# Q and k chunks of pairs 1 and 2 as block products ahead of attention, half the fill pieces, and a new order inside an attention step

## The chip, the cores and the metric

The kernel runs on one core of a Trainium2 chip, in one launch. The metric is the device time in microseconds; the kernel before took 1108.95 us, the median of three runs (1108.9 to 1109.0).

## What is computed

One layer of a trunk over x (1024 tokens, 1024 features, float32): a token mixer, then a SwiGLU network, each between two RMS norms with a residual. Cut to the part around the change:

```python
h = rms_norm(x, g_pre_mix)
hc, bg, cg, q, k, v = split(h @ w_in, 6)          # each 1024 tokens x 512
y_conv = bg * causal_conv3(cg * hc)               # 512 channels
y_attn = band_attention(q, k, v, rel_bias)        # 8 heads of 64, chunks of 64 tokens,
                                                  # each sees itself and 8 chunks to the left
y = [group_norm(y_conv), group_norm(y_attn)] @ w_out
x = x + rms_norm(y, g_post_mix)
x = x + rms_norm((silu(gate) * up) @ w_ffn_out, g_post_ffn)   # gate, up from rms_norm(x) @ w_ffn_in
```

## The kernel before

Every float32 operand of a large product is split into a high part (rounded to the matmul's format, by ScalarE) and a low part (the rest, by VectorE), and a product takes three passes: high x high, high x low, low x high. A chunk is 128 output channels for all 1024 tokens, so plainly it takes 8 slices of the contraction x 3 passes x 2 halves of the tokens = 48 matmuls of 512 columns.

**Stages.** First v is projected, while the normed x is transposed. Then come FRONT = 6 rounds (`front_multiply`). A round makes two chunks at once with seven block products in place of eight (a Strassen-Winograd scheme: the 2 x 2 blocks are the two chunks' weights in two halves of the contraction, and the even and odd token tiles in two halves of it). A block product is 12 matmuls, a round 84, where two plain chunks take 96. The sums of weights (`front_sum`) and of results (`bank_sum`: u2, u3, c22, c21, c12) are VectorE's; ScalarE makes the high parts (`front_high`), VectorE the low ones (`front_low`). Rounds 0 to 4 make the conv's inputs and gates, round 5 q and k of head pair 0. Conv statistics and transposes of three conv channels groups (`stats`, `norms`) lie between products of rounds 4 and 5. Then comes the attention of four pairs of heads, t = 0 to 3 (PAIRS = 4, LAST = 3), then the output projection, the FFN in block products, and the end.

**The attention.** A pair has 9 steps (s = 0 to STEPS - 1), and 8 tiles of 128 queries. The band of a tile has up to 640 keys (tiles 4 to 7; fewer for the first ones). A unit u is one head of a tile. For each tile:

- TensorE `scores(t, i)`: q times k in three passes, both heads side by side in the array, into PSUM.
- VectorE `add_bias(t, u)`: adds the bias, takes the maximum, writes scores to SBUF (`biased` counts units).
- ScalarE `exp(t, u)`: the exponential and its sum (`exp_done`).
- TensorE `transpose_p(t, i)`: the weights turned, into PSUM; ScalarE `read_pT` copies them to SBUF (`pT_act`), for 640 keys VectorE copies the fifth block (`pT_dve`).
- TensorE `output(t, i)`: tiles i and i + 1 times v, after both are copied; VectorE `copy_o`, TensorE `turn_back`, VectorE `read_o` bring them to their place. ScalarE `squares` sums squares of o for its norm, `o_norm`, `o_scale`, `o_finish` and `transpose_o` finish the norm one pair later.

Each engine's queue is written out by hand in its own `step(t, s)`, and works in that order. A wait holds all that stands behind it on its engine.

**Fill.** The q and k chunks of pairs 1 to 3 and two chunks of the conv's last group (c and b) are not made in rounds but in 64 pieces of 6 matmuls (`piece`), laid between the steps of the attention: AHEAD = 3 before the first step, and FILLS per step. Four pieces make half a chunk, in one PSUM bank. `half_bank()` is free again when a reader has copied the half out (`read_half`, semaphores `half_free`), so the first piece of a half waits for that copy. ScalarE copies halves of q and k into rows QN and KN, VectorE multiplies the conv's into CU and CV. `high_in` and `low_in` split the weights of the next chunk, `high_q`, `low_q`, `high_k`, `low_k` split the next pair's q and k for its scores (`qk_ready`).

**Queues.** SP issues the loads of weights (`load_front`, `load`), the stores and loads of v (`store_v`, `load_v`) and of the three finished conv groups (`store_conv`, `load_conv`), in program order, each behind its semaphore. GpSimd's queue brings the bias and raises the norms' means to the power -1/2.

TensorE's step before, cut:

```python
if s in (3, 5, 7):
    output(t, s - 3)
if scored(t, s):
    pe.wait_ge(biased, unit(t, 2 * s))
    for i in scored(t, s):
        scores(t, i)
...
pe.wait_ge(exp_done, unit(t, 2 * s))
transpose_p(t, s - 1)
for q in range(pieces_ahead(t, s), pieces_ahead(t, s + 1)):
    piece(q)
```

## Time and profile before

| | |
|---|---|
| median of 3 runs | 1108.95 us |
| the profiled execution | 1108.85 us, span of its instructions 1106.8 us |
| granted clock of TensorE | 1.00 over the span |
| TensorE busy | 1096.4 us, 99% of the span, 5653 matmuls recorded |
| VectorE, ScalarE, GpSimd busy | 764.7, 480.4, 160.4 us |
| chain that ended last | TensorE 97%, ScalarE 1%, DMA 1% |
| DMA | 164.11 MB, mean 148 GB/s |

The span is what the rows' times count in; the execution's own time is 2.05 us longer. A busy time of TensorE counts matmuls from start to a modelled end, which overlap, so the distance between two starts tells what one costs. The chain is followed back from the last instruction; since it is TensorE nearly throughout, the time is TensorE's work and its waits. The rounds lie from 60.28 to 183.40 us, the attention from there to 367.30.

### The profile page before, as it was taken

To read this page: it belongs to the slowest core of one execution; us is meant where nothing else is said; L and a number is where in the kernel's file an instruction comes from. 1 tells how busy PE (TensorE), PEld (TensorE's weight loads), DVE (VectorE), ACT (ScalarE), POOL (GpSimd) and SP (SyncE) were. 2 spreads that over 40 slices of the span, in tenths; PEclk is the share of its full clock that TensorE was granted. 3 is DMA by queue.
4 is the path that set the end of the run, shared out by engine and by line. 5 is a ranking of instruction groups with operands and counts; after the bars stand their busy time and mean duration, and the time that the engine had idled before them with its cause. 6 is when DMAs were issued, how large, how long until landed. Compare 5 with 4: busy or idle time off the path is not lost.

```text
span 1106.8 us, 16172 instructions
## 1 busy us (share of the span) xinstructions
PE 1096.4 (99%) x5653; PEld 908.6 (82%) x5653; DVE 764.7 (69%) x1267; ACT 480.4 (43%) x911; POOL 160.4 (14%) x258
## 2 busy tenths in 40 slices
PE   8999999999999999999999999999999999999997
PEld 7888887878878888888888888888888888888886
DVE  6878855455656756868777777878787777555584
ACT  6542233666665655734323232323223257444441
POOL 2300022010101220312112211211221110000031
PEclk9999999999999999999999999999999999999999
DMA  7332216300100444535546445543644689677632
GB/s 273 110 119 71 58 57 230 113 20 21 38 2 20 160 163 135 171 96 172 159 145 208 135 123 187 177 146 114 218 136 150 212 304 385 235 232 223 219 115 79
DMA packets 116183, 164.11 MB, mean 148 GB/s; under 512 B 7752, under 2 KB 73304, under 8 KB 116128
## 3 DMA queue, kind: packets, MB, share of 16 engines
q1 hardware_dynamic: 98496, 103.30, 29.2%
q0 software_dynamic: 16464, 55.89, 14.5%
q10 hardware_dynamic: 1168, 4.20, 1.0%
q8 instruction: 33, 0.54, 0.2%
q14 instruction: 22, 0.18, 0.1%
HBM read 119.56 MB, written 46.94 MB: 150 GB/s over the span
## 4 chain that ended last, share of the span: by engine, by line
PE 97%; ACT 1%; DMA 1%; DVE 0%; issue 0%; SPq 0%; DVEq 0%; POOL 0%; POOLq 0%
PE psum L1280 34%; PE psum L1307 18%; PE psum L874 12%; PE psum L1113 10%; PE psum L1164 8%; PE psum L1025 4%; PE psum L917 3%; PE psum L898 2%; PE psum L888 2%; PE psum L863 1%; PE psum L1001 1%; DMA arena<-in_x 1%; PE psum L925 0%; PE psum L1007 0%; PE psum L907 0%; ACT arena L1516 0%
## 5 line engine op out<-in xcount | busy, mean ns | idle before, releaser
L1280 PE MATMUL psum<-arena_r,ws 128*128 128x512 f32 x960 | 224.1, 389 | 0.0
L1280 PEld LDWEIGHTS psum<-arena_r,ws 128*128 128x128 f32 x960 | 180.3, 188 | 37.3
L1280 PE MATMUL psum<-hT,ws 128*128 128x512 f32 x720 | 169.9, 389 | 0.0
L1280 PEld LDWEIGHTS psum<-hT,ws 128*128 128x128 f32 x720 | 135.1, 188 | 27.9
L874 PE MATMUL psum<-hT,ws 128*128 128x512 f32 (+1 forms) x624 | 142.3, 380 | 0.4 <-ACT arena L1542 0.4
L1307 PE MATMUL psum<-hT 128*128 128x512 f32 (+1 forms) x600 | 135.2, 385 | 0.0
L1307 PEld LDWEIGHTS psum<-hT 128*128 128x128 f32 x600 | 111.3, 188 | 22.5
L874 PEld LDWEIGHTS psum<-hT,ws 128*128 128x128 f32 x624 | 107.9, 189 | 20.0 <-issue 0.8
L2401 DVE TENSOR_TENSOR misc<-misc,psum 128x512 f32<-128x512 f32 x100 | 68.4, 684 | 49.1 <-PE psum L1280 45.7
L1724 ACT ACTIVATE ws<-o_raw 128x512 fp32r<-128x512 f32 x40 | 25.1, 627 | 139.2 <-DVE o_raw L2379 138.7
L1164 PE MATMUL psum<-ws,hT 128*128 128x512 f32 x348 | 81.7, 393 | 0.0
L1307 PE MATMUL psum<-ws 128*128 128x512 f32 (+1 forms) x348 | 78.1, 382 | 0.0
L1164 PEld LDWEIGHTS psum<-ws,hT 128*128 128x128 f32 x348 | 64.5, 188 | 13.5 <-issue 0.3
L1307 PEld LDWEIGHTS psum<-ws 128*128 128x128 f32 x348 | 63.9, 188 | 12.6
L1724 ACT ACTIVATE ws<-raw 128x512 fp32r<-128x512 f32 x80 | 49.7, 623 | 39.2 <-PE psum L1280 38.3
L1113 PE MATMUL psum<-arena_r,ws 128*128 128x512 f32 x276 | 65.5, 391 | 0.0
L1113 PEld LDWEIGHTS psum<-arena_r,ws 128*128 128x128 f32 x276 | 51.4, 188 | 10.6
L2396 DVE TENSOR_TENSOR ws<-raw,ws 128x512 fp32r<-128x512 f32 x80 | 55.1, 690 | 6.7
L2475 DVE TENSOR_TENSOR hT<-arena,hT 128x512 fp32r<-128x512 f32 x62 | 40.0, 687 | 19.9 <-ACT hT L1771 19.5
L1357 ACT ACTIVATE misc<-arena 128x1024 bf16<-128x1024 f32 (+2 forms) x37 | 34.8, 941 | 40.8 <-DVE arena L2527 16.6
L1771 ACT ACTIVATE hT<-arena 128x512 fp32r<-128x512 f32 x62 | 35.6, 624 | 36.8 <-PE psum L1307 29.8
L1113 PE MATMUL psum<-hT,ws 128*128 128x512 f32 x216 | 51.2, 390 | 0.0
(262 smaller groups left out, 1578.0 us busy)
## 6 DMA issues: line engine op xcount, KB each, us to landing
raw<-in_w_ffn_in SPq DMA_DIRECT2D x44, 512.0 KB, 4.4
act_scratch<-arena POOLq DMA_DIRECT2D x77, 256.0 KB, 3.2
raw<-in_w_in SPq DMA_DIRECT2D x22, 512.0 KB, 3.9
arena<-in_w_ffn_out POOLq DMA_DIRECT2D x22, 512.0 KB, 5.7
arena<-act_scratch SPq DMA_DIRECT2D x38, 256.0 KB, 3.5
arena<-in_x SPq DMA_DIRECT2D x16, 512.0 KB, 6.7
raw<-in_w_out SPq DMA_DIRECT2D x16, 512.0 KB, 3.3
raw<-act_scratch SPq DMA_DIRECT2D x26, 256.0 KB, 3.2
```

The costliest lines, as they stand in the source:

```text
L874: last = mm(PP[pair][:, at:end] if to is None else to, w[wp], hT[:, hp, k, at:end], start=(k == 0 and (wp, hp) == (0, 0)), stop=(k == KT - ...
L1025: last = mm(v_bank(i), hT[:, hp, k, i * P:(i + 1) * P], v_weights(wp, k), start=(k == 0 and part == 0), stop=k == 7 and part == (1 if i < ...
L1113: last = mm(blocks(front_bank(n, i)), w[:, k * P:(k + 1) * P], b_operand(i, part, k), start=fresh_bank and k == 0 and w is hi and part == ...
L1164: last = mm(pair[:, half * 512:(half + 1) * 512], a, ws[:, slot, wp, half * 512:(half + 1) * 512], start=(first is not None and a is hi an ...
L1280: last = mm(blocks(bank), w[:, k * P:(k + 1) * P], b_operand(i, part, k), start=fresh_bank and k == 0 and w is hi and part == 0, stop=k == ...
L1307: last = mm(bank[:, at:end], a[:, n * P:(n + 1) * P], b[:, at:end], start=fresh_bank and a is ah and b is bh, stop=i == NP - 1 and a is al ...
L1357: go(dst, src, ACT.Square, scale=scale, accum_out=acc).then_inc(done[0], 1)
L1724: go(w_op(i)[0], w_raw[i], ACT.Copy).then_inc(w_hi, 1)
L1771: go(out_op(c, part)[0], raw_ring[c % RING][:, part * 512:(part + 1) * 512], ACT.Copy).then_inc(out_hi, 1)
L2396: tt(lo, w_raw[i], hi.bitcast(F32), ALU.subtract).then_inc(w_split, 1)
L2401: tt(out, a, bank, ALU.add).then_inc(made, 1)
L2475: tt(lo, raw_ring[c % RING][:, part * 512:(part + 1) * 512], hi.bitcast(F32), ALU.subtract).then_inc(out_split, 1)
```

## The change

- FRONT_PAIRS = 3: q and k of pairs 1 and 2 are made in two more rounds, in the order pair 2, pair 1, pair 0 (FRONT = 8). Their results are staged in rows 18 and 17: ScalarE stages one block (`stage_c11`), VectorE writes the other three; SP stores them to DRAM (`store_qk`) and reads them back, behind v, into rows of their own (`load_qk`, QK_ROWS).
- FILLED = 4 chunks are left for fill: q and k of pair 3, and the conv's last c and b. That is 32 pieces: AHEAD = 4, none in steps 0 to 2 of pairs 0 and 1, none in steps 0 and 1 of pairs 2 and 3.
- TensorE's step: scores stand first; the output of two tiles behind them; the last output of a pair moves behind the next pair's first scores; in step 8 the fill stands ahead of the transposes.
- ScalarE's step: the exps of the step's own tile stand ahead of the copy of the previous tile's weights; a half of a chunk is copied (`drain`) at the end of the step after its last piece. Squares stay at the same kind of place for tiles 0 and 1 of a pair (step 5) and for the others move with the later output.
- VectorE's step: the bias of the step's own tile stands first, `copy_o` and `read_o` behind it; its halves and the taps of the conv's last group follow `drain`.
- The three conv groups come back from DRAM only when pair 3's q and k are split.

```diff
+    FRONT_PAIRS = 3
+    FILLED = 2 * (PAIRS - FRONT_PAIRS) + 2
+    OUT0 = FILLED
...
-    FRONT = 6
+    FRONT = 5 + FRONT_PAIRS
...
+            def store_qk(n):
+
+                t = FRONT - 1 - n
+                for part, done in enumerate((c12_made, c21_made)):
+                    sp.wait_ge(done, n + 1)
+                    at = (2 * t + part) * P
+                    sp.dma_start(qk_d[at:at + P, :], row(QK_STAGED[part])).then_inc(qk_stored, 16)
...
-        AHEAD = 3
-        FILLS = [[1] + [2] * 7 + [1]] * LAST + [[1] + [2] * 4 + [1] * 4]
+        AHEAD = 4
+        FILLS = [[0, 0, 0, 1, 1, 1, 1, 1, 1]] * 2 + [[0, 0, 1, 1, 1, 1, 1, 1, 2]] * 2
...
+        def halves_done(t, s):
+
+            return [h for h in range(2 * FILLED) if step_of(4 * h + 3) == STEPS * t + s - 1]
```

TensorE's step, ScalarE's step and VectorE's step:

```diff
             def step(t, s):
                 if s == 0:
                     pe.wait_ge(qk_ready, t * 2 + 2)
-                if s == 3 and t == 0:
-                    pe.wait_ge(v_back, 64)
-                if s in (3, 5, 7):
-                    output(t, s - 3)
                 if scored(t, s):
                     if unit(t, s) > 0:
                         pe.wait_ge(biased, unit(t, 2 * s))
                     for i in scored(t, s):
                         scores(t, i)
                 if s == 0 and t > 0:
-                    turn_back(t - 1, NT - 2)
+                    output(t - 1, NT - 2)
+                if s == 3 and t == 0:
+                    pe.wait_ge(v_back, 64)
+                if s in (3, 5, 7):
+                    output(t, s - 3)
...
+                if s == NT and t < LAST:
+                    fill(t, s)
                 if s > 0:
                     pe.wait_ge(exp_done, unit(t, 2 * s))
-                    if s in (2, 4):
+                    if s > 1:
                         pe.wait_ge(pT_act, tile(t, s - 1))
...
                     transpose_p(t, s - 1)
+                    if s == 1 and t > 0:
+                        turn_back(t - 1, NT - 2)
```

```diff
             def step(t, s):
                 more = t < LAST
                 if s == 0:
-                    exp(t, 0)
-                    exp(t, 1)
-                    return
-                if more and s in (1, 3):
-                    read_half(2 * t, QN, s // 2)
-                if more and s in (5, 7):
-                    read_half(2 * t + 1, KN, (s - 5) // 2)
+                    drain(t, s)
+                    exp(t, 0), exp(t, 1)
+                    if t > 0:
+                        squares(t - 1, (4, 5))
                 if more and s == 7:
                     high_q(t)
-                read_pT(t, s - 1)
-                if s < NT:
-                    exp(t, 2 * s)
-                    exp(t, 2 * s + 1)
...
+                if 0 < s < NT:
+                    exp(t, 2 * s), exp(t, 2 * s + 1)
...
+                if s == 5:
                     if t > 0:
                         act.wait_ge(o_var, t)
                     squares(t, (0, 1))
...
+                if s > 0:
+                    read_pT(t, s - 1)
+                    drain(t, s)
+                if s == 1 and t > 0:
+                    squares(t - 1, (6, 7))
+                for g in chunks_next(t, s):
+                    high_in(g)
```

```diff
+                if s == NT and more:
+                    low_k(t)
                 if s < NT:
                     add_bias(t, 2 * s)
                     add_bias(t, 2 * s + 1)
+                if s == 0 and t > 0:
+                    copy_o(t - 1, NT - 2)
+                if s == 1 and t > 0:
+                    read_o(t - 1, NT - 2)
...
+                if s in (3, 5, 7):
+                    copy_o(t, s - 3)
...
+                drain(t, s)
+                for g in chunks_next(t, s):
+                    low_in(g)
```

**The order at three places.** TensorE's queue from the end of the rounds, pair 0, before and now (the 512-column rows from hT are fill, 256 to 512 columns from ws are scores, rows from ident transposes, 64x128 rows the output):

```order
L874 MATMUL psum<-hT,ws 128x512 x18
L888 MATMUL psum<-ws 128x256 x6
L874 MATMUL psum<-hT,ws 128x512 x6
L888 MATMUL psum<-ws 128x256 x6
L898 MATMUL psum<-ident,misc 128x128 x2
L874 MATMUL psum<-hT,ws 128x512 x12
L888 MATMUL psum<-ws 128x384 x6
L888 MATMUL psum<-ws 128x512 x6
L898 MATMUL psum<-ident,arena 128x128 x4
L874 MATMUL psum<-hT,ws 128x512 x12
L917 MATMUL psum<-misc,arena 64x128 x2
```

```order
L927 MATMUL psum<-hT,ws 128x512 x24
L941 MATMUL psum<-ws 128x256 x12
L951 MATMUL psum<-ident,misc 128x128 x2
L941 MATMUL psum<-ws 128x384 x6
L941 MATMUL psum<-ws 128x512 x6
L951 MATMUL psum<-ident,arena 128x128 x4
L970 MATMUL psum<-misc,arena 64x128 x2
L970 MATMUL psum<-arena 64x128 x4
L951 MATMUL psum<-ident,misc 128x128 x6
L978 MATMUL psum<-ident,arena 128x128 x2
L927 MATMUL psum<-hT,ws 128x512 x6
```

The second tile's scores now follow the first's directly, and from there to the transposes of tile 2 no fill is left.

ScalarE's queue at the opening of pair 1, before and now (128x128 to 128x640 with `biased` are exps, `pT_psum` rows copy turned weights, 128x64 rows are squares, `half_used` or `chunk_used` rows from psum copy a half):

```order
L1516 ACTIVATE misc,lsum<-misc,nmax 128x128 [waits biased] x2
L1542 ACTIVATE arena<-psum 128x512 [waits half_used]
L1525 ACTIVATE misc<-psum 128x2x128 [waits pT_psum]
L1516 ACTIVATE arena,lsum<-arena,nmax 128x256 [waits biased] x2
L1349 ACTIVATE ws<-raw 128x1024 [waits chunk_used,raw_landed1]
L1532 ACTIVATE sq_junk,osq<-o_raw 128x64 [waits o_sq,tile_free] x4
L1525 ACTIVATE arena<-psum 128x2x256 [waits pT_psum]
L1516 ACTIVATE misc,lsum<-misc,nmax 128x384 [waits biased] x2
```

```order
L1602 ACTIVATE misc,lsum<-misc,nmax 128x128 [waits biased] x2
L1618 ACTIVATE sq_junk,osq<-o_raw 128x64 [waits o_sq,tile_free] x4
L1602 ACTIVATE arena,lsum<-arena,nmax 128x256 [waits biased] x2
L1611 ACTIVATE misc<-psum 128x2x128 [waits pT_psum]
L1618 ACTIVATE sq_junk,osq<-o_raw 128x64 [waits o_sq,tile_free] x4
L1602 ACTIVATE misc,lsum<-misc,nmax 128x384 [waits biased] x2
L1611 ACTIVATE arena<-psum 128x2x256 [waits pT_psum]
L1602 ACTIVATE arena,lsum<-arena,nmax 128x512 [waits biased] x2
```

The half and the high part of a chunk left this place, four squares more came to it, and each copy of weights stands behind the exps of the next tile.

ScalarE's queue in steps 4 and 5 of pair 1, before and now:

```order
L1525 ACTIVATE arena<-psum 128x2x512 [waits pT_psum]
L1516 ACTIVATE misc,lsum<-misc,nmax 128x640 [waits biased] x2
L1349 ACTIVATE ws<-raw 128x1024 [waits chunk_used,raw_landed0]
L1542 ACTIVATE arena<-psum 128x512 [waits half_used]
L1525 ACTIVATE misc<-psum 128x2x512 [waits pT_psum]
L1516 ACTIVATE arena,lsum<-arena,nmax 128x640 [waits biased] x2
L1532 ACTIVATE sq_junk,osq<-o_raw 128x64 [waits o_sq,tile_free] x4
```

```order
L1602 ACTIVATE misc,lsum<-misc,nmax 128x640 [waits biased] x2
L1611 ACTIVATE arena<-psum 128x2x512 [waits pT_psum]
L1602 ACTIVATE arena,lsum<-arena,nmax 128x640 [waits biased] x2
L1618 ACTIVATE sq_junk,osq<-o_raw 128x64 [waits o_sq,tile_free,o_var]
L1618 ACTIVATE sq_junk,osq<-o_raw 128x64 [waits o_sq,tile_free] x3
L1611 ACTIVATE misc<-psum 128x2x512 [waits pT_psum]
L1628 ACTIVATE arena<-psum 128x512 [waits half_used]
```

The copy of the half went from ahead of the weights and exps to behind exps, squares and weights.

## Rows read from the trace of the kernel before

**Rows 1.** Page, part 1: busy time of each engine and share of the span
```profile
PE 1096.4 (99%) x5653; PEld 908.6 (82%) x5653; DVE 764.7 (69%) x1267; ACT 480.4 (43%) x911; POOL 160.4 (14%) x258
```
**Rows 2.** Windows, the attention: length, busy us of each engine, granted clock, DMA share, GB/s
```profile
183.40:367.30 183.90, 182.33 (x1447) 147.89 (x1446) 102.40 (x339) 113.06 (x307) 9.54 (x5) 1.00 0.17 57
```
**Rows 3.** Timeline of PE in two rounds; last row: windows, the round between them
```profile
109.64 5.60 PE L1113 MATMUL psum<-arena_r,ws 128*128 128x512 f32 x24
...
128.68 5.60 PE L1113 MATMUL psum<-arena_r,ws 128*128 128x512 f32 x24
...
109.64:128.68 19.04, 19.04 (x85) 15.77 (x84) 15.22 (x22) 5.17 (x9) 0.00 (x0) 1.00 0.20 56
```
**Rows 4.** Timeline of PE, pair 0's opening: start us, us, engine, line, operation, count
```profile
183.40 4.24 PE L874 MATMUL psum<-hT,ws 128*128 128x512 f32 x18
187.57 0.62 PE L888 MATMUL psum<-ws 64*128 64x256 f32 x6
...
189.72 0.63 PE L888 MATMUL psum<-ws 64*128 64x256 f32 x6
...
193.62 1.49 PE L888 MATMUL psum<-ws 64*128 64x384 f32 x12
...
195.45 3.01 PE L874 MATMUL psum<-hT,ws 128*128 128x512 f32 x12
```
**Rows 5.** Timeline of PE, last steps of pair 3
```profile
352.01 1.09 PE L898 MATMUL psum<-ident,arena 128*128 128x128 f32 x8 [0.25 <-ACT arena L1516]
...
353.07 1.64 PE L874 MATMUL psum<-hT,ws 128*128 128x512 f32 x6
354.64 1.31 PE L917 MATMUL psum<-misc,arena 128*64 128x128 f32 x20
...
356.98 1.16 PE L888 MATMUL psum<-ws 64*128 64x384 f32 x12
358.07 1.09 PE L898 MATMUL psum<-ident,misc 128*128 128x128 f32 x8
...
359.35 1.62 PE L874 MATMUL psum<-hT,ws 128*128 128x512 f32 x6
...
362.33 1.09 PE L898 MATMUL psum<-ident,arena 128*128 128x128 f32 x8 [0.48 <-ACT arena L1516]
```
**Rows 6.** Timeline of DVE, bias in pair 0's opening and in a full step
```profile
189.38 0.15 DVE L2133 TENSOR_SCALAR nmax<-omax 128x1 f32<-128x1 f32 x1
...
191.90 0.15 DVE L2133 TENSOR_SCALAR nmax<-omax 128x1 f32<-128x1 f32 x1
...
256.09 0.82 DVE L2129 CUSTOM_DVE_ANT_0 arena<-psum,arena 128x640 f32<-128x640 f32 x1 [0.34 <-issue]
...
258.14 0.15 DVE L2133 TENSOR_SCALAR nmax<-omax 128x1 f32<-128x1 f32 x1
```
**Rows 7.** Timeline of ACT: exps, weights (L1525), squares (L1532), a half (L1542)
```profile
197.33 0.19 ACT L1516 ACTIVATION_READ_ACCUMULATOR misc<-misc,nmax 128x1 f32 x1
...
235.35 0.60 ACT L1542 ACTIVATE arena<-psum 128x512 f32<-128x512 f32 x1 [0.20 <-PE psum L874]
...
257.53 1.03 ACT L1525 ACTIVATE misc<-psum 128x1024 f32<-128x1024 f32 x1 [2.89 <-PE psum L907]
...
259.26 0.82 ACT L1516 ACTIVATE arena<-arena,nmax 128x640 f32<-128x640 f32 x1
259.99 0.19 ACT L1516 ACTIVATION_READ_ACCUMULATOR arena<-arena,nmax 128x1 f32 x1
260.08 0.24 ACT L1532 ACTIVATE sq_junk<-o_raw 128x64 f32<-128x64 f32 x1
...
261.56 0.19 ACT L1532 ACTIVATION_READ_ACCUMULATOR sq_junk<-o_raw 128x1 f32 x1
```
**Rows 8.** Timeline of SP, then the DMA view of it: last column us to landing
```profile
183.49 0.49 SPq L577 DMA_DIRECT2D arena<-value_scratch  x1
...
arena<-value_scratch SPq DMA_DIRECT2D x1, 512.0 KB, 12.5
```

More of the change, by code:

```diff
@@ L622, in _ @@
                 load(g % 2, wout_d[m * P:(m + 1) * P, :])
+                if g == OUT0 + 1:
+                    sp.wait_ge(qk_ready, 2 * PAIRS)
+                    for t in range(PAIRS - 1):
+                        load_conv(t)
                 if g == OUT0 + 4:
@@ L975, in step, with fill @@
                     transpose_p(t, s - 1)
+                    if s == 1 and t > 0:
+                        turn_back(t - 1, NT - 2)
                     if s == 1 and t > 1:
-                        pe.wait_ge(tile_free, tile(t, 0) + 1)
-                        transpose_o(t - 1, OT_BANKS)
+                        last_half = pieces_ahead(t, s) // 4 - 1
+                        pe.wait_ge(half_free[last_half % 2], last_half // 2 + 1)
+                        pe.wait_ge(o_ready, t - 1)
+                        for i in range(NT):
+                            last = tr(OT_BANKS[:, i // 4, i % 4 * P:(i % 4 + 1) * P], row(CR, P, i * P), ident[:, :])
+                        last.then_inc(oT_psum, 1)
+                if s < NT or t == LAST:
+                    fill(t, s)
+                if s == NT and t == LAST:
+                    output(t, NT - 2)
+            def fill(t, s):
                 for q in range(pieces_ahead(t, s), pieces_ahead(t, s + 1)):
                     piece(q)
-                if s == NT:
-                    output(t, NT - 2)
             def copied(t, i):
@@ L2083, in _ @@
             conv_mix(0)
-            front_low(5, 6)
+            front_low(5, 5)
             make_c12(4)
             times(2, 1, u2).then_inc(front_out, 1)
-            make_u2(5)
-            conv_mix(1)
-            make_u3(5)
-            conv_stats_read(2)
-            front_low(5, 5)
+            front_low(5, 6)
+            for n in range(5, FRONT - 1):
+                q_row, k_row = [row(r) for r in QK_STAGED]
+                make_u2(n)
+                front_low(n + 1, 0)
+                if n == 5:
+                    conv_mix(1)
+                    conv_stats_read(2)
+                make_u3(n)
+                front_s(n + 1)
+                front_low(n + 1, 1), front_low(n + 1, 2)
+                if n == 5:
+                    dve.wait_ge(conv_stored[1], 16)
+                else:
+                    dve.wait_ge(qk_stored, 32 * (n - 5))
+                make_c22(n, tiles_of(k_row, 1), 1)
+                front_low(n + 1, 3), front_low(n + 1, 4)
+                make_c21(n, tiles_of(k_row, 0), 0)
+                front_low(n + 1, 5)
+                if n == 5:
+                    conv_mix(2)
+                    dve.wait_ge(conv_stored[0], 16)
+                bank_sum(n, 6, tiles_of(q_row, 1), blocks(u2), blocks(BANK[3]), c12_made)
+                front_low(n + 1, 6)
+            n = FRONT - 1
+            make_u2(n)
+            make_u3(n)
             low(1, 0, 0)
-            make_c22(5)
-            conv_mix(2)
+            make_c22(n)
             nc.vector.memset(gate[:, :], 0.0).then_inc(tile_free, 1)
@@ L2158, in read_half @@
                     dve.wait_ge(half_used, g + 1)
-                out = row(CV if j else CU, HALF, at)
+                out = row(CU if g == CG else CV, HALF, at)
                 tt(out, half_bank(), row(CV, HALF, at), ALU.mult).then_inc(half_free[half], 1)
@@ L2197, in step @@
                     add_bias(t, 2 * s + 1)
+                if s == 0 and t > 0:
+                    copy_o(t - 1, NT - 2)
+                if s == 1 and t > 0:
+                    read_o(t - 1, NT - 2)
+                if s == 1 and t > 1:
+                    o_finish(t - 1, OT_BANKS)
+                if s == 2 and t > 0:
+                    o_norm(t)
+                if s in (3, 5, 7):
+                    copy_o(t, s - 3)
+                if s == 7 and more:
+                    low_q(t)
@@ L2210, in step @@
-                if s == 2 and t > 0:
-                    o_norm(t)
-                if more and s == 4:
-                    low_in(2 * t + 2)
-                if more and s == 7:
-                    low_q(t)
-                if not more and s == 3:
-                    tap(t, 0)
-                if not more and s == 4:
-                    tap(t, 1), tap(t, 2)
-                if not more and s == 7:
+                if s == 4:
+                    if t > 0:
+                        o_scale(t)
+                    read_o(t, 0)
```

207 lines of the change are left out of this document (119 added, 88 removed).

## The prediction

> **What bounds the kernel now.** I read the page first: TensorE is busy for 1096.4 of the span of 1106.8 us [rows 1], so a change counts by what it does to TensorE's work and to its waits. Then the stretch of the attention, from its first matmul at 183.40 to the first of the output projection at 367.30: 183.90 us, 182.33 of them busy, so only 1.57 us of waiting [rows 2]. Last the timeline of the three engines there, for the durations and for the distance between a score and its softmax. The point to see in it is that this distance is long (about 4 us) and that the fill pieces now hide it.
>
> **What the change removes and adds on TensorE.** Rounds run without a gap: from the first product of one at 109.64 to that of the next at 128.68 is 19.04 us for 84 matmuls, 0.2267 each [rows 3]. Two more rounds add 168 matmuls, 38.1 us. Of the 64 fill pieces of six matmuls, 32 go: 192 matmuls, 43.5 us. Net, 24 matmuls less, -5.4 us. A stretch of fill costs 0.21 us over its matmuls (six take 1.57 from 353.07 to 354.64, against 6 x 0.2267 = 1.36) [rows 3, 5]. Beside the opening one there were 36 such stretches, one a step; there are now 23 (five, five, six and seven), since openings have none and step 8's joins step 7's: 13 less, -2.7 us. So TensorE's own work falls by 8.1 us.
>
> The Trainium skill (TensorE: Matmul & The Clock Gate, on the back-to-back issue gap) has streams of 512-column matmuls at about 131 ns each; by that the 24 would be worth only 3.1 us. The rows' 226.7 ns is the one that applies.
>
> **What the new rounds cost elsewhere.** VectorE was busy for 15.22 of the 19.04 us of a round that also had taps and gates, ScalarE for 5.17, and TensorE had no gap [rows 3]; the new rounds have neither taps nor gates, only q's and k's staging, so I cost them at nothing. SP issues four stores and four loads of 512 KB more, the stores behind the next round's weights and long before their readers, the loads behind v, and needed only in step 7 of pair 0. The conv rows now come back only once pair 3's q and k are split, some 35 us before their first use; such a transfer took up to 12.5 us in the densest stretch [rows 8]. Both are hidden; without that cover a transfer would cost its few us, which the upper end holds. The rows of v are read at the same place before the end of the last round; the last landed 12.5 us after its issue at 183.49, so 12.6 after the end of the rounds [rows 8]. TensorE needs them at 11.8 in the new order, and waits until 13.8 for another reason (below), so they cost nothing, with 1 us of slack.
>
> **What is late once the fill is gone.** I count from the end of the rounds (183.40 before), with these durations. TensorE: fill 1.57, output of two full tiles 2.34 (354.64 to 356.98), scores 1.09, an even tile's transposes 1.28, an odd one's 1.07 [rows 5]. VectorE: both heads' bias of 640 keys 2.20 (256.09 to 258.14 + 0.15) [rows 6]. ScalarE: an exp 0.91 (259.26 to 259.99 + 0.19), a tile's weights out of PSUM 1.0, squares of two tiles 1.7 (260.08 to 261.56 + 0.19), half a chunk 0.6 (235.35) [rows 7]. Handing over takes about 0.1.
>
> *Pair 0's opening.* The three pieces took 187.57 - 183.40 = 4.17; a fourth makes it 5.53 [rows 4]. Scores of tile 0 start then; their bias was done 1.96 after such a start (189.38 + 0.15 - 187.57), so tile 1's start at 7.6 rather than 6.1: **1.5 us** of waiting. Those were followed by their bias after 2.33 (191.90 + 0.15 - 189.72), which tiles 2 and 3 wait for: 10.0 rather than 8.6, **1.4**. Scores and transposes take 1.83 (193.62 to 195.45), to 11.8. The output of tiles 0 and 1 needs tile 1's weights copied, and ScalarE now does tile 2's exps first: these end 3.90 after the start of the scores (197.33 + 0.19 - 193.62) less the copy of about 0.5 that stood ahead of them, then 0.6 for the copy: 13.8, **2.0** [rows 4, 6, 7]. Before, 12 matmuls of fill lay in each of these places.
>
> *Every step with full tiles.* From the end of a step's scores, the bias is done at 2.3, the second exp at 3.3, and the copy, now behind it, at 4.3. TensorE comes to the output that needs the copy after odd transposes, one piece and the next scores: 3.5. **0.8** in step 5 of each pair, **0.6** in step 7 of the first two. Behind even transposes nothing waits.
>
> *A piece that opens a half of a chunk.* There is one PSUM bank for the halves, and a half is now copied out at the end of the next step, behind exps and weights. Transposes end, the weights take 1.3, the half 0.6: about **1.9** in step 7 of pair 0; in step 5 of pair 1 four squares stand before it as well: **3.0**; in step 6 of pairs 2 and 3 it is VectorE's, behind two biases: **2.3** each.
>
> *The openings of pairs 1 to 3.* The previous pair's last output now stands behind the scores: it waits 0.5 for its weights and its copy delays turning back by 0.3. VectorE has that copy ahead of the bias of tile 1, so tiles 2 and 3 score late: **1.2** in pair 1; in pair 2 VectorE also waits there for ScalarE's high part of the last filled chunk, behind four squares: **2.8**; in pair 3 a tap lies there: **1.8**. Then the output of tiles 0 and 1 waits for the copy of tile 1 behind squares and exps: **2.5**; in pair 2, with one piece now in step 2, **1.0**; in pair 3, with two taps and an o chunk on VectorE ahead of tile 2's bias, **3.5**.
>
> Sums: pair 0 1.5 + 1.4 + 2.0 + 0.8 + 0.6 + 1.9 = 8.2; pair 1 0.8 + 1.2 + 2.5 + 0.8 + 3.0 + 0.6 = 8.9; pair 2 0.8 + 2.8 + 1.0 + 0.8 + 2.3 = 7.7; pair 3 1.1 + 1.8 + 0.2 + 3.5 + 0.8 + 2.3 = 9.7. Together 34.5 us, where 1.6 were. The attention then takes 183.9 - 46.2 (43.5 + 2.7) + 32.9 = 170.6 us.
>
> **The sum.** +38.1 - 46.2 + 32.9 = +24.8 us. On the profiled execution's own 1108.85 us (span 1106.8) that is 1133.7; the median of the runs, 1108.95, is 0.1 above it, so I say 1134. The handovers and the order in which small tasks end may move each of some 20 waits by 0.3 us, mostly together: 1127 to 1141 for this case.
>
> **The rivals.**
> 1. *Only the openings wait.* The waits of the openings are chains that rows show end to end; those of full steps and of halves (0.8 + 0.6 + 1.9 + 0.8 + 3.0 + 0.6 + 0.8 + 2.3 + 0.8 + 2.3 = 13.9) hang on where squares, copies and halves meet in two queues, and are differences of long sums. If they don't come about: 1133.7 - 13.9 = 1119.8. Against it: in pair 3 before, with one piece a step as now, TensorE already waited, 0.25 and 0.48 us, for exps [rows 5].
> 2. *The steps cover themselves* (the other side). The scores stand first, so bias and exp run beside output and transposes; if each of 26 steps then waits only like those two rows of pair 3, at the lower of them, 26 x 0.25 = 6.5 replaces the 1.6: 1108.85 - 8.1 + 4.9 = 1105.7, faster. It decides at 9.7 us of waiting in all; below that the change gains. Against it: pair 0's opening alone has 4.9, and nothing of another tile's work stands there to fill it.
> 3. *The clock falls.* The granted clock was 1.00, the higher level of 2.4 GHz, all through the attention, with waits under 0.5 us [rows 2, 5]; seven of my waits are of 2 us or more. If after the four of 2.5 us or more the next step (scores, transposes, fill: 3.7 us) ran at 1.2 GHz, twice as long, that is 15 us more: 1149. The Trainium skill (TensorE: Matmul & The Clock Gate, Part 1) says that idle TensorE goes back to the lower clock; no row here shows one long enough.
> 4. *A transfer or a staging row is late.* v, or the q and k rows, could each hold TensorE for 1 to 4 us: 1135 to 1138, inside my range.
>
> **How the numbers follow.** Chances: my forecast 0.62, openings only 0.18, steps that cover themselves 0.07, the clock 0.09, late transfers 0.04. The range leaves out the clock and the faster rival: from 1119, just under the openings' case, to 1145, above it by the upper ends of the own range and of a late transfer. A measurement of this kernel tells 0.2% (2.2 us) from no change; faster by more than that holds most of rival 2, 0.06; within it 0.02; slower 0.92.
>
> **What would show it.** In the changed profile: the two rounds at 19.04 us each without gaps; some 171 us from the last product to the output projection; TensorE idle some 30 to 35 us there, before the scores of tiles 1 and 2 and the output of tile 0 (on VectorE's bias and ScalarE's copy), before step 5's output, and before the fill that opens a half (0.8 to 3 us, on ScalarE's or VectorE's copy of a half); the clock at 1.00. I would be wrong if TensorE's idle time there were under 20 us, if a round had gaps, or if the clock showed the lower level.

## The result and the profile after

The changed kernel takes **1137.51 us** (median of 4 runs, 1135.72 to 1138.46), the kernel before 1108.93 us beside it: a ratio of 1.0256, 95% interval 1.0243 to 1.0268. It is slower by 28.6 us; forecast were 25 and a time of 1134 us. The profiled execution has 1138.04 us, its span 1136.0.

The page of the changed kernel: busy time as in [rows 1], then TensorE's granted clock in 40 slices.

```profile
PE 1098.4 (97%) x5629; PEld 911.2 (80%) x5629; DVE 783.0 (69%) x1295; ACT 484.1 (43%) x917; POOL 160.2 (14%) x258
...
PEclk9999999989989999999999999999999999999999
```

TensorE issues 24 matmuls fewer and is yet busy for 2.0 us more. The clock row says where to look: two slices have an 8 in them, both in the attention.

Windows of the changed kernel (columns as in [rows 2]): the two new rounds, the attention, then five stretches inside it.

```profile
183.25:221.33 38.08, 38.08 (x170) 31.53 (x168) 18.88 (x29) 10.05 (x16) 1.81 (x3) 1.00 0.42 137
221.33:396.27 174.94, 147.48 (x1255) 120.05 (x1253) 98.37 (x335) 107.32 (x297) 9.75 (x6) 0.94 0.18 61
230.46:240.75 10.29, 8.40 (x40) 6.67 (x41) 4.58 (x24) 5.81 (x15) 0.00 (x0) 0.50 0.99 335
290.36:297.23 6.87, 6.40 (x46) 5.00 (x46) 2.76 (x11) 2.80 (x6) 0.00 (x0) 1.00 0.00 0
312.49:315.60 3.11, 3.11 (x15) 2.36 (x16) 2.86 (x10) 2.75 (x13) 0.00 (x0) 0.50 0.38 149
336.20:339.60 3.40, 3.40 (x24) 2.71 (x24) 0.84 (x3) 0.92 (x1) 0.00 (x0) 0.51 0.00 0
363.50:366.90 3.40, 3.40 (x12) 2.53 (x10) 0.17 (x1) 1.30 (x3) 0.61 (x1) 0.51 0.02 5
```

The two rounds' 168 products take 38.08 us and have no gap; the attention starts at 221.33 where it started at 183.40 [rows 2], 37.9 us later. It takes 174.94 us instead of 183.90: 34.9 us of work went (182.33 to 147.48), and 25.9 us of idle time came (1.57 to 27.46). In four stretches, some 20 us together, the granted clock is 0.50, the lower level of 1.2 GHz.

The timeline of TensorE in pair 0's opening and in its later steps, the answer to [rows 4] (a bracket gives the idle time ahead of the row and, behind the arrow, what ended it):

```profile
221.33 5.60 PE L927 MATMUL psum<-hT,ws 128*128 128x512 f32 x24
226.86 0.62 PE L941 MATMUL psum<-ws 64*128 64x256 f32 x6
228.88 0.62 PE L941 MATMUL psum<-ws 64*128 64x256 f32 x6 [1.40 <-DVE nmax L2249]
...
231.61 2.61 PE L941 MATMUL psum<-ws 64*128 64x384 f32 x12 [1.75 <-DVE nmax L2249]
234.15 1.12 PE L951 MATMUL psum<-ident,arena 128*128 128x128 f32 x4
236.00 0.69 PE L970 MATMUL psum<-misc,arena 128*64 128x128 f32 x4 [0.73 <-issue]
...
246.75 0.88 PE L970 MATMUL psum<-misc,arena 128*64 128x128 f32 x12 [0.68 <-ACT arena L1611]
...
262.15 3.01 PE L927 MATMUL psum<-hT,ws 128*128 128x512 f32 x12 [1.69 <-ACT arena L1628]
```

The scores of tile 1 and those of tiles 2 and 3 wait for VectorE's bias, 1.40 and 1.75 us, where fill stood before. The second of these rows takes 2.61 us for what took 1.49 at the full clock [rows 4]. The output of step 5 waits for the copy of the weights (L1611), the fill that opens a half for the copy of the half before it (L1628).

ScalarE's timeline at the first output, the copy of tile 1's weights behind the exps of tile 2, as forecast:

```profile
235.22 0.19 ACT L1602 ACTIVATION_READ_ACCUMULATOR misc<-misc,nmax 128x1 f32 x1
235.32 0.58 ACT L1611 ACTIVATE arena<-psum 128x512 f32<-128x512 f32 x1
```

TensorE's timeline again, in pairs 1 to 3, the long waits:

```profile
275.85 0.44 PE L970 MATMUL psum<-misc,arena 128*64 128x128 f32 x4 [2.06 <-ACT arena L1611]
...
290.36 1.60 PE L927 MATMUL psum<-hT,ws 128*128 128x512 f32 x6 [2.71 <-ACT arena L1628]
...
312.49 2.61 PE L941 MATMUL psum<-ws 64*128 64x384 f32 x12 [2.13 <-DVE nmax L2249]
...
362.25 0.44 PE L970 MATMUL psum<-misc,arena 128*64 128x128 f32 x4 [3.48 <-ACT arena L1611]
```

### The profile page after: what moved, and what is told of

Read it like the earlier page. It is cut to its first block, busy times and chain, and to the rows that moved or that the text cites. A ratio compares the mean times of both kernels' runs of the same rounds, so it can differ in the third digit from the quotient of the medians.

```text
span 1136.0 us, 16219 instructions
## 1 busy us (share of the span) xinstructions
PE 1098.4 (97%) x5629; PEld 911.2 (80%) x5629; DVE 783.0 (69%) x1295; ACT 484.1 (43%) x917; POOL 160.2 (14%) x258
## 4 chain that ended last, share of the span: by engine, by line
PE 65%; DVE 0%; ACT 0%; issue 0%; POOL 0%; DVEq 0%; POOLq 0%
PE psum L1346 34%; PE psum L1373 18%; PE psum L1230 8%; PE psum L927 4%; PE psum L916 1%; PE psum L970 0%; PE psum L951 0%; PE psum L1060 0%; PE psum L1067 0%; DVE arena L2708 0%; ACT misc L1423 0%; PE psum L941 0%; DVE arena L2648 0%; PE psum L1073 0%; DVE arena L2643 0%
## 5 line engine op out<-in xcount | busy, mean ns | idle before, releaser
L1346 PE MATMUL psum<-arena_r,ws 128*128 128x512 f32 x960 | 224.1, 389 | 0.0
L1346 PEld LDWEIGHTS psum<-arena_r,ws 128*128 128x128 f32 x960 | 180.2, 188 | 37.4
L1346 PE MATMUL psum<-hT,ws 128*128 128x512 f32 x720 | 169.9, 389 | 0.0
L1346 PEld LDWEIGHTS psum<-hT,ws 128*128 128x128 f32 x720 | 135.1, 188 | 28.0
L927 PE MATMUL psum<-hT,ws 128*128 128x512 f32 (+1 forms) x432 | 97.0, 378 | 8.6 <-ACT arena L1628 4.4
L927 PEld LDWEIGHTS psum<-hT,ws 128*128 128x128 f32 x432 | 74.3, 193 | 21.7 <-issue 9.4
L1179 PE MATMUL psum<-arena_r,ws 128*128 128x512 f32 x372 | 88.2, 391 | 0.0
L1179 PEld LDWEIGHTS psum<-arena_r,ws 128*128 128x128 f32 x372 | 69.4, 188 | 14.3
L1179 PE MATMUL psum<-hT,ws 128*128 128x512 f32 x288 | 68.2, 390 | 0.0
L1179 PEld LDWEIGHTS psum<-hT,ws 128*128 128x128 f32 x288 | 53.9, 188 | 11.8 <-DVE ws L2048 0.7
```

What stands on the lines that cost most here:

```text
L927: last = mm(PP[pair][:, at:end] if to is None else to, w[wp], hT[:, hp, k, at:end], start=(k == 0 and (wp, hp) == (0, 0)), stop=(k == KT - ...
L1179: last = mm(blocks(front_bank(n, i)), w[:, k * P:(k + 1) * P], b_operand(i, part, k), start=fresh_bank and k == 0 and w is hi and part == ...
L1346: last = mm(blocks(bank), w[:, k * P:(k + 1) * P], b_operand(i, part, k), start=fresh_bank and k == 0 and w is hi and part == 0, stop=k == ...
```

## The experiments

Beside "waits" stands TensorE's idle time in the attention (its length less the busy time, from the windows). The runs of before on the same chips had medians of 1108.84 to 1108.94 us.

The text calls *cover* the fill that lies where TensorE would wait.

**1. The copies of halves first.** The changed kernel; `drain` stands at the start of each step of ScalarE and VectorE.

```diff
 def step(t, s):
+    drain(t, s)
...
-        read_pT(t, s - 1)
-        drain(t, s)
+        read_pT(t, s - 1)
```

> The changed kernel (1137.5 us) with one thing moved: a finished half of a chunk is copied out of its PSUM bank at the start of the next step on ScalarE and VectorE, not at the end. My theory: the four waits of TensorE before the fill that opens a half (1.69, 2.71, 2.10, 2.10 us in the changed kernel's trace) come from the copy's place in the queue, so nearly all of 8.6 us goes, with perhaps one of the stretches at the lower clock: 1127 to 1130. Rival: one PSUM bank for the halves is the cause, and the waits stay whatever the place: 1136 to 1138.

Measured: 1126.06 us (1.0154, 1.0137 to 1.0171), 11.4 us less than the changed kernel and a little below the range expected. The attention:

```profile
221.33:384.76 163.43, 143.76 (x1255) 118.03 (x1255) 98.48 (x335) 106.70 (x297) 9.95 (x7) 0.96 0.19 67
```

The four waits ahead of fill (1.69, 2.71, 2.10, 2.10, together 8.6) are gone; waiting falls from 27.5 to 19.7 us. Busy time falls by 3.7 as well, since the clock is low for a shorter time: in three stretches of some 14 us together (6.8 us from 232.9, 3.4 from 273.9, 3.6 from 348.9), where it was 20. So these waits cost what their rows show and some of the clock. Most waits of the openings stayed; in pair 0 the first output waits 1.22 for 0.73, new ones of 0.61 (pair 1, ahead of scores), 0.84 and 0.57 (pair 2, ahead of outputs) and 0.60 (pair 3) came, and in pair 3 the 1.15 and 3.48 became one of 2.56.

**2. The weights' copy ahead of the exps.** The changed kernel with the old place of `read_pT` on ScalarE alone.

```diff
+                if s > 0:
+                    read_pT(t, s - 1)
                 if 0 < s < NT:
                     exp(t, 2 * s), exp(t, 2 * s + 1)
...
-                    read_pT(t, s - 1)
                     drain(t, s)
```

> The changed kernel with ScalarE's copy of the previous tile's weights put back ahead of the exps of the step's own tile. My theory: the six waits before outputs of full tiles (0.46 to 0.68 us, 3.6 in all) and part of those before the output of tiles 0 and 1 go, but the exps then end later, behind a copy that itself waits for the transposes, and TensorE waits before transposes instead: net 0 to 4 us, 1133.5 to 1137.5. Rival: this order is the main cause of the loss: 1125 or less.

Measured: 1144.93 us (1.0323, 1.0306 to 1.034), 7 us slower than the changed kernel: both expectations failed. TensorE's timeline, then ScalarE's at the same place:

```profile
263.97 4.58 PE L927 MATMUL psum<-hT,ws 128*128 128x512 f32 x12 [4.25 <-ACT arena L1628]
```

```profile
259.76 1.02 ACT L1611 ACTIVATE misc<-psum 128x1024 f32<-128x1024 f32 x1 [2.64 <-PE psum L960]
...
262.21 0.19 ACT L1602 ACTIVATION_READ_ACCUMULATOR arena<-arena,nmax 128x1 f32 x1
262.30 1.04 ACT L1649 ACTIVATE ws<-arena 128x1024 fp32r<-128x1024 f32 x1
263.25 0.58 ACT L1628 ACTIVATE arena<-psum 128x512 f32<-128x512 f32 x1
```

ScalarE now idles 2.64 us for the transposes, and the exps, which were ready, run only behind that copy; so the half comes later still, and TensorE waits 4.25 us instead of 1.69. The waits of the attention rise by 3.6 us (31.1 for 27.5) and its busy time by 4.2 (151.6 for 147.5), at a clock of 0.93 for 0.94. So the change's place for this copy fits its order on TensorE; of the two places tried, that of the half was the bad one.

**3. TensorE kept busy in pair 0's opening.** 45 transposes of the identity into the idle half bank in steps 0 to 2 of pair 0; nothing reads them.

```diff
+            WARM = {(0, 0): 12, (0, 1): 15, (0, 2): 18}
...
+                for _ in range(WARM.get((t, s), 0)):
+                    tr(PP[3][:, HALF:HALF + P], ident[:, :], ident[:, :])
```

> The changed kernel with 45 idle transposes of the identity laid into TensorE's waits of pair 0's opening (steps 0 to 2), whose results nobody reads. My theory: the waits there brought the clock down to half for 10.3 us (230.5 to 240.8), and that costs about 2.7 us; with the transposes the clock stays at 1.00 there, the waits for bias and weights show as before or longer, and the time falls by 2 to 3.5 us to 1134 to 1135.5. Rival: the fall has nothing to do with the waits, or it costs nothing because the chain through VectorE and ScalarE sets the pace there: 1137 to 1139.

Measured: 1136.37 us (1.0248, 1.0231 to 1.0265), between the two expectations. That is 1.1 us less than the changed kernel, whose interval overlaps with this one, so the times show no gain; the traces show what happened. Windows of this run: the opening, all of pair 0 to the output of step 5, and a later stretch; then the row of the changed kernel for the second of these.

```profile
230.00:240.00 10.00, 9.89 (x87) 8.22 (x85) 4.90 (x24) 5.72 (x15) 0.00 (x0) 1.00 1.03 346
221.33:244.27 22.94, 22.00 (x164) 17.85 (x162) 11.05 (x48) 10.69 (x26) 1.09 (x4) 1.00 0.84 300
290.30:293.50 3.20, 3.20 (x17) 2.24 (x16) 0.04 (x2) 0.00 (x0) 0.00 (x0) 0.51 0.02 5
```

```profile
221.33:246.75 25.42, 20.86 (x120) 16.04 (x118) 11.12 (x48) 10.79 (x26) 1.02 (x3) 0.80 0.77 271
```

The clock stayed at 1.00 in the opening, and the same work was done 2.5 us sooner (22.94 against 25.42), although the changed kernel is busy at half the clock for 8.40 us there, which would be 4.2 us more. The rest was waiting for bias and copies in either case. Of the 2.5 us, 1.5 were lost later: behind the opening this profile has four low stretches (from 273.3, 290.3, 314.3 and 361.9) and the changed kernel's three. The one at 290.3 came after the wait of 2.7 us before pair 1's half, where the clock had held in the changed kernel's profile.

**4. Pieces in the openings.** The changed kernel with 32 pieces laid otherwise.

```diff
-        FILLS = [[0, 0, 0, 1, 1, 1, 1, 1, 1]] * 2 + [[0, 0, 1, 1, 1, 1, 1, 1, 2]] * 2
+        FILLS = [[1, 1, 1, 0, 1, 0, 1, 0, 1], [1, 0, 1, 0, 1, 0, 1, 0, 1],
+                 [1, 0, 2, 0, 2, 0, 1, 1, 2], [0, 0, 2, 0, 2, 0, 1, 0, 3]]
```

> The changed kernel with the same 32 pieces at other steps: one or two pieces in steps 0, 1 or 2 of each pair, few in steps 3, 5 and 7, and seldom a half that opens in the step after another has ended. My theory: what counts is whether a piece lies where bias, exps and copies are awaited; the openings' waits (some 13 us) and the half waits (8.6) mostly go, and with them the low clock (some 9 us): TensorE idle under 12 us in the attention, 1110 to 1117. Rival: 32 pieces are too few wherever they lie, since full steps without a piece wait as much as the openings did: 1127 or more.

Measured: 1122.27 us (1.012, 1.0103 to 1.0137), between the two expectations. Waits are 16.8 us. TensorE's timeline: pair 0's opening, and tile 5's transposes in pairs 1 and 2, behind a step that gave up its piece.

```profile
227.58 1.63 PE L927 MATMUL psum<-hT,ws 128*128 128x512 f32 x6 [0.23 <-ACT arena L1628]
...
231.87 1.49 PE L941 MATMUL psum<-ws 64*128 64x384 f32 x12 [0.35 <-DVE nmax L2249]
...
284.00 1.06 PE L951 MATMUL psum<-ident,arena 128*128 128x128 f32 x8 [1.15 <-ACT misc L1611]
...
321.46 1.06 PE L951 MATMUL psum<-ident,arena 128*128 128x128 f32 x8 [1.43 <-ACT misc L1611]
```

Pair 0's opening waits 0.23 and 0.35 instead of 1.40 and 1.75, so a piece there does what it did before. But the transposes of tile 5, behind step 5 without a piece, now wait 0.85 to 1.43 us in every pair. The longest waits are 2.08 us ahead of scores in pair 0 and 2.11 ahead of pair 3's first output, both followed by a low clock. The 32 pieces are fewer than the places that want one.

**5. Both of these.** Halves first, and pieces in the openings (FILLS as in run 4, with one piece moved from step 7 of pair 2 to step 0 of pair 3).

> The run with the 32 pieces in the openings (1122.3 us) and the half copied first (which alone gave 1126.1), together; one piece moves from step 7 of pair 2 to step 0 of pair 3. If the two undo the same waits, as I hold (with the pieces in the openings a half seldom opens right after another's end), the gains don't add: 1118 to 1122. Rival: they are separate costs and add, 1137.5 - 11.4 - 15.2 = 1110.9.

Measured: 1122.55 us (1.0119, 1.0104 to 1.0135), half a microsecond above my own range and far from the rival's. The gains of 11.4 and 15.2 us together give 15.0: with the pieces in the openings no fill waited over 0.23 us for a half any more (run 4; one transpose of o did, 1.30 us), so little was left for the other edit to take away.

**6. One pair ahead.** FRONT_PAIRS = 2, so one new round and 48 pieces, in the new order, halves first.

> Only pair 1's q and k made in a round ahead (seven rounds), 48 pieces of fill instead of 32, nearly all steps with one or two, halves copied first. TensorE's own work is then between the two kernels: 12 matmuls fewer than in the kernel before, -2.7 us, and about ten stretches of fill fewer, -2 us. If the amount of cover sets the waits, they should fall to 4 to 8 us (1.6 before, 27 in the changed kernel) and the clock stay up: 1106.5 to 1112, no clear difference from the kernel before. Rival: the new order of a step costs by itself, whatever the cover: 1115 or more.

Measured: 1120.9 us (1.0112, 1.0096 to 1.0127), its rival's side. Waits are 14.4 us, among them one of 3.13 us before pair 1's first output, behind the copy of the weights:

```profile
259.15 0.44 PE L970 MATMUL psum<-misc,arena 128*64 128x128 f32 x4 [3.13 <-ACT arena L1611]
```

**7. The same with the weights' copy ahead of the exps.** Runs 6 and 2 together.

> The same seven rounds and 48 pieces, with ScalarE's copy of the previous tile's weights ahead of the exps. With the changed kernel's thin cover this order lost 7 us more. My theory: with thicker cover it takes away the wait before outputs (0.7 us, six times) and gives part of it back before transposes: within 2 us of the run without it, 1106 to 1112. Rival: it loses again by several us, so the order of the kernel before needs its whole fill.

Measured: 1131.25 us (1.0195, 1.0181 to 1.0209), 10 us slower than run 6, the rival's side. Waits are 18.7 us for 14.4, and the busy time is 168.8 for 162.7 at a clock of 0.96 for 0.99. With run 2 this shows twice that the place of this copy costs 7 to 10 us in the new order, a good half of it by the clock.

**8. The kernel before, with the exps first.** All 64 pieces and all else as before; only ScalarE's two calls change places, and TensorE's wait that this calls for.

```diff
-                    if s in (2, 4):
+                    if s > 1:
                         pe.wait_ge(pT_act, tile(t, s - 1))
...
-                read_pT(t, s - 1)
                 if s < NT:
                     exp(t, 2 * s)
                     exp(t, 2 * s + 1)
+                read_pT(t, s - 1)
```

> The kernel before (1108.9 us), with ScalarE's exps of the step's own tile ahead of the copy of the previous tile's weights, and the wait for that copy ahead of each transpose, as in the changed kernel; all 64 pieces stay. My theory: 12 matmuls of fill a step cover the later copy: 1108.5 to 1110.5. Rival: the order costs by itself, the 0.5 to 0.7 us before each output of the changed kernel appear here too, and more in the openings: 1112 or more.

Measured: 1113.12 us (1.0041, 1.0027 to 1.0054), the rival's side: with full cover this part of the new order costs 4.2 us by itself. Waits rise from 1.6 to 5.6 us:

```profile
208.15 0.88 PE L917 MATMUL psum<-misc,arena 128*64 128x128 f32 x12 [0.41 <-ACT arena L1525]
...
358.84 1.31 PE L917 MATMUL psum<-misc,arena 128*64 128x128 f32 x20 [1.32 <-ACT arena L1525]
```

**9. The old order with 32 pieces.** The changed kernel's rounds, with the steps of before on TensorE, ScalarE and VectorE, halves first, and pieces in the openings (FILLS [1,1,1,1,0,1,0,2,0] and the like).

> The changed kernel's block products and its 32 pieces, with the step of the kernel before on TensorE, ScalarE and VectorE (output and transposes' place, halves drained first), and about one piece in each of the first four steps of a pair. By the sum of the prediction the rounds cost 38.1 us and the fill and the stretches give back 46.2, so with no new wait at all 1101 us would be left. Theory A (the order inside a step has a price of its own, some 4 us with full cover, more with thin cover, as the runs of one pair ahead and of the exps first showed): with the old order 1109 to 1119 us, so faster than the same pieces in the new order (1122.5) by 3 us or more. Theory B (only the number of pieces that cover the waits counts): 1121 to 1124 us, as the new order with pieces in the openings.

Measured: 1127.56 us (1.0168, 1.0153 to 1.0184). Both expectations failed: the old order is 5 us slower than the new one with 32 pieces (run 5), not faster. The pieces do not lie alike in the two, so this is a bound on what order can give and no measure of it. Waits are 21.9 us, the longest before outputs, whose copy the old order asks for earlier:

```profile
281.53 0.88 PE L970 MATMUL psum<-misc,arena 128*64 128x128 f32 x12 [2.13 <-ACT arena L1602]
...
365.51 0.88 PE L970 MATMUL psum<-misc,arena 128*64 128x128 f32 x12 [2.13 <-ACT arena L1602]
```

**10. The old order with 48 pieces.** As run 9 with FRONT_PAIRS = 2 and FILLS [1,1,2,2,1,1,1,2,0], [1,1,1,2,1,2,1,2,0], [1,1,1,2,1,2,1,1,1], [1,1,1,2,1,1,1,2,1].

> The old step order with pair 1 alone as block products, 48 pieces, one or two of them in each step but one. Without a new wait: half of the gain, 1108.9 + 19.0 - 21.8 - 1.3 = 1104.8 us. Theory A (order has its own price, cover is enough at 48): 1105 to 1110 us, at least 11 us faster than the same pieces in the new order (1120.9). Theory B (cover is what is short): 1116 us or more.

Measured: 1113.87 us (1.0051, 1.0037 to 1.0065), between the two, and 7 us faster than the new order with 48 (run 6). The attention, with the clock at 1.00 and 9.1 us of waits, and its longest wait:

```profile
202.19:372.16 169.97, 160.92 (x1352) 130.30 (x1350) 99.89 (x337) 108.67 (x301) 9.79 (x7) 1.00 0.18 60
```

```profile
288.24 1.31 PE L970 MATMUL psum<-misc,arena 128*64 128x128 f32 x20 [2.41 <-ACT arena L1602]
```

**11. The old order with the change's own pieces.** It differs from run 1 by the order of the steps alone.

> The old step order with the changed kernel's own table of pieces (none in steps 0 and 1 of a pair), halves drained first; it differs from the run with the halves first (1126.1 us) by the order alone. Theory A (order has a price): 1116 to 1122 us. Theory B (the openings without a piece set it, whatever the order): 1124 to 1128 us. A third case: the old order, made for steps that all have a piece, waits longer where they have none: above 1130 us.

Measured: 1127.85 us (1.0169, 1.0154 to 1.0185), as theory B has it: at the same 32 pieces in the same steps the orders differ by 1.8 us, and the intervals of the ratios overlap.

**12. The old order, 48 pieces laid by the trace of run 10.** Steps 7 and 8 of every pair get two and one.

```diff
+        FILLS = [[1, 1, 1, 1, 1, 1, 2, 2, 1], [1, 1, 1, 2, 1, 1, 2, 2, 1],
+                 [1, 1, 1, 1, 1, 1, 1, 2, 1], [1, 1, 1, 1, 1, 2, 1, 2, 1]]
```

> The run with the old order and 48 pieces (1113.9 us, waits of 8.9 us in the attention against 1.6), with the pieces laid where its trace waited: in its steps 7 and 8, pair 3 has two and one pieces and waits 0.26 us, pairs 0 to 2 have two and none or one and one and wait 1.1, 2.4 and 2.7. Now all pairs have two and one there, and the pieces come from steps 2 to 5. Without any wait it would be 1104.8 + 1.6 = some 1106 us. If the waits hang on which step has the cover, those 5 us go and little comes in their place: 1108 to 1110.5 us, at best the kernel before. If the sum of the cover is what is short, waits of the same size turn up in steps 2 to 5: 1112 to 1115 us.

(The 1106 in it adds the 1.6 us twice; 1104.8 has them already.) Measured: 1114.61 us (1.005, 1.0036 to 1.0064), no better than run 10, as the second expectation has it. Of the waits that it was laid against, pair 0's 1.1 is gone and pair 1's 2.4 has become 1.02, but pair 2's 2.7 is still 2.37, and two new ones of 0.74 and 0.75 came in step 5, in which or ahead of which a piece was taken:

```profile
287.34 1.31 PE L970 MATMUL psum<-misc,arena 128*64 128x128 f32 x20 [1.02 <-ACT arena L1602]
...
305.89 0.88 PE L970 MATMUL psum<-misc,arena 128*64 128x128 f32 x12 [0.74 <-ACT arena L1602]
...
318.00 1.31 PE L970 MATMUL psum<-misc,arena 128*64 128x128 f32 x20 [2.37 <-issue]
```

Waits are 8.2 us for 9.1: they moved. So at 48 pieces the sum of the cover seems to be what is short; one other table is no proof that none does better.

**The runs side by side**, all times in us; pieces are those left as fill, waits and clock those of the attention.

| run | pieces | step order | waits | clock | time |
|---|---|---|---|---|---|
| before | 64 | old | 1.6 | 1.00 | 1108.9 |
| 8 | 64 | old, exps first | 5.6 | 1.00 | 1113.1 |
| 10 | 48 | old | 9.1 | 1.00 | 1113.9 |
| 12 | 48 | old, laid by run 10's trace | 8.2 | 1.00 | 1114.6 |
| 6 | 48 | new, halves first | 14.4 | 0.99 | 1120.9 |
| 4 | 32 | new, openings | 16.8 | 0.98 | 1122.3 |
| 5 | 32 | new, halves first, openings | 17.2 | 0.98 | 1122.6 |
| 1 | 32 | new, halves first | 19.7 | 0.96 | 1126.1 |
| 9 | 32 | old, openings | 21.9 | 0.97 | 1127.6 |
| 11 | 32 | old, the change's own pieces | 21.3 | 0.97 | 1127.9 |
| 7 | 48 | new, halves and weights first | 18.7 | 0.96 | 1131.3 |
| 3 | 32 | new, 45 idle transposes | 23.8 | 0.96 | 1136.4 |
| the change | 32 | new | 27.5 | 0.94 | 1137.5 |
| 2 | 32 | new, weights first | 31.1 | 0.93 | 1144.9 |

No version beats the kernel before. By the counts, 16 pieces turned into a round should take some 4 us off TensorE (19.0 for a round against 21.8 and a part of the stretches). Run 10, with the clock at 1.00 throughout, shows 2.6: its attention starts 18.8 us later (202.19 for 183.40) and is busy for 21.4 us less (160.92 for 182.33). The change shows 6.1 for two rounds, the clock's 9.2 us (below) left out. With 48 pieces the waits are already 7.5 us longer.

## Why the prediction came out right, step by step

- **Two rounds, +38.1.** Measured 37.9, without a gap. Staging, stores and loads of q and k cost TensorE nothing there, and no wait of TensorE in the attention was for v or the q and k rows: the last load of v was issued at 220.42 and took at most 12.4 us to land, so it was there by 233, and its reader started at 236.00. The 0.73 us ahead of that one has no releaser in its row; ScalarE's copy of the weights, which it reads, ended at 235.90 (235.32 + 0.58).
- **32 pieces and 13 stretches gone, -46.2.** The counts agree (1447 records to 1255 in the attention, 192 fewer). The busy time fell by 34.9 only; the clock and the tails below are the difference.
- **The waits, 34.5 forecast.** The rows add to 27.3, the window says 27.5. By pair, forecast and measured: 8.2 and 6.7; 8.9 and 7.3; 7.7 and 5.3; 9.7 and 8.0. Place for place most agree: bias in pair 0's opening 1.5 and 1.4 forecast, 1.40 and 1.75 measured; step 5's output 0.8 and 0.68; the halves 1.9, 3.0, 2.3, 2.3 and 1.69, 2.71, 2.10, 2.10; pair 3's output 3.5 and 3.48. Nearly every wait lies where it was put, with the releaser that was named. What failed is size, by chains added up with each handover at its full length: the outputs behind the first scores of pairs 1 to 3 (0.8, 0.8, 1.1 and 0.44, 0.44, 0.56 with the turning back), pair 2's openings 2.8 and 2.13, and its 1.0 not there at all, pair 3's 1.8 and 1.15, its 0.2 not there. The 1.1 and 0.2 stand in the sum without a working. Pair 0's first output is another case, 2.0 and 0.73: TensorE's own scores and transposes ahead of it ran at half the clock and took 1.8 us more, so it came later to the same copy. At full clock, in run 3, that output began 3.97 us behind the start of those scores, and the prediction had 3.8 (its own terms, 3.90 less 0.5 and plus 0.6, add to 4.0). So 1.3 of the 7 us that the waits fell short are the clock's doing too.
- **The clock, held to be at 1.00.** This failed, and the prediction had named it as a sign of being wrong. It was the third rival, at 0.09, and came partly true beside the forecast. Busy time at the lower level was 8.40 + 3.11 + 3.40 + 3.40 = 18.3 us, half of which, 9.2, is lost to the clock. Run 3 shows that of pair 0's 4.2 only 2.5 counted. So the clock cost some 7 to 8 us where the waits were 7 too few, and the two errors nearly cancel. That the time came out within 4 us is in part luck: the rounds, the pieces and the places of the waits were understood, the clock was not. The rival's own price, 15 us, was twice too high: it had four steps of 3.7 us each fall with their full time added, and the low stretches outside pair 0 last 3.1 to 3.4 us, so each adds about 1.7.
- **The rest, 2.2 us.** TensorE was busy for 147.5 us where 136.1 were forecast; 9.2 are the clock. What remains I put down to the ends of matmuls, which no next one overlaps where the engine then waits; that is argued from the 23 waits there and not shown by a run.
- **The sum.** +37.9 for the rounds and -9.0 for the attention (183.90 to 174.94) are +28.9, against 28.6 between the medians; forecast were +38.1 - 13.3 = +24.8. The whole error of 4 us lies in the attention, 174.9 for 170.6.
- **Openings only (0.18) and steps that cover themselves (0.07)** both fell: step 5's outputs and the halves waited as worked out (13.9 forecast, 12.2 by their rows), and the waits in all were nearly three times the 9.7 us that would have decided for a gain.

On the clock, the Trainium skill (TensorE: Matmul & The Clock Gate, Part 1) has idle TensorE go back to the lower clock. The rows at 0.50 agree in so far as they begin inside the wait of 1.75 us, at the end of that of 2.13, and some 1.2 us behind those of 2.10 and 3.48; the wait of 2.71 us did not bring it down in this profile.

My beliefs on the cause, beyond the sum, did worse. I thought that 48 pieces would bring the waits down to 4 to 8 us in the new order too (run 6: 14.4 us, and 9 us slower than the range), that the copy of the weights stood wrongly (runs 2 and 7: moved, it costs 7 to 10 us), and that the old order would be better with 32 pieces too (run 9: it is not). What holds over all runs is narrower: few pieces leave waits in either order. Full cover favours the old order by 4.2 us (run 8, for the exps' place alone), 48 pieces by some 7, and at 32 the two are level (runs 1 and 11) or the new one is ahead (runs 5 and 9). As the tables of pieces differ in the pairs of runs with 48 pieces and in runs 5 and 9, how much of those differences is the order's stays open. Also open is which mix of waits brings the clock down.

## What to carry to other kernels

Work that stands between a result and its use is not only work. Here each 16 pieces moved out of the attention were some 3 us cheaper on TensorE, and each lost more than that in waits of 0.7 to 3.5 us; before moving filler ahead, count the places that need one and the length of the softmax chain (score to copied weights, some 4 us here), and compare with what is left. When a step's order is changed along with it, the small tasks behind it need new places too: the one copy of a half, moved to the end of its step, was 11.4 of the 28.6 us. And a wait may be priced by more than its row: three of the four times that the clock fell here were at waits of over 2 us, though as many such waits left it as it was.

## What the runs showed of the hardware

- The granted clock fell to 0.50 inside an attention that is 84% busy, at waits of 1.75 to 3.48 us. Three of the four stretches in the changed kernel's profile lasted 3.1 to 3.4 us; the first, with waits of 1.40, 1.75 and 0.73 us close together, lasted 10.3.
- It was not the same in every run: a wait of 2.71 us at 290.36 left the clock at 1.00 in the changed kernel, and the same wait at 289.40 in run 3 (2.72 us, before the same instruction) was followed by 0.51. In run 6 a wait of 3.13 us at 259.15 left it at 1.00, and one of 2.10 at 348.46 was followed by a low stretch. The profiles of before and of runs 8, 10 and 12 have no low stretch; their longest wait is run 10's 2.41 us. The runs of the changed kernel spread over 2.7 us, those of before over 0.1, and this fits it.
- Low stretches came both with the DMA engines full (share 0.99 at 230.46) and with them idle (0.00 at 336.20), so the traffic is not what brought them.
- With 45 identity transposes in the waits of an opening the clock stayed at 1.00 and the opening was 2.5 us shorter; tile 1's scores began 0.2 us later (2.22 us behind tile 0's for 2.02).
